# Alternating the high-part and low-part products of the expert weights, k by k, in a streaming-encoder kernel

## The reference, cut to what matters

```python
def peer_ffn(h, w_q, sub_keys, u_tab, v_tab):
    ...
        idx = jnp.take_along_axis(cand_i, best_pos, axis=-1)
        gate = jax.nn.softmax(best_s, axis=-1)
        u = jnp.take(u_tab, idx, axis=0)
        act = jax.nn.gelu(jnp.einsum('td,thkd->thk', hb, u).astype(F32))
        v = jnp.take(v_tab, idx, axis=0)
        return jnp.einsum('thk,thkd->td', (gate * act).astype(hb.dtype), v)
```

## Time and profile before

| | |
|---|---|
| time, median of 3 runs | 1838.51 us (1835.72 to 1839.15) |
| span of the profiled execution | 1830.5 us |
| PE busy | 1796.4 us, 98% of the span |
| DVE busy | 1476.1 us, 81% |
| ACT busy | 1115.6 us, 61% |
| POOL busy | 769.2 us, 42% |
| mean granted TensorE clock | 0.999 of full |
| DMA | 391.70 MB, mean 214 GB/s |

### The profile page before, as it was taken

How to read it: one execution, slowest core, us unless ns; L and a number is a source line. 1 busy time by engine, 2 the same in 40 slices (tenths; PEclk the granted TensorE clock), 3 DMA queues, 4 the chain that set the end, 5 groups by cost and what they waited for, 6 DMA issues and landing times. The chain is left out here.

```text
span 1830.5 us, 38340 instructions
## 1 busy us (share of the span) xinstructions
PE 1796.4 (98%) x11836; PEld 1695.5 (93%) x11836; DVE 1476.1 (81%) x3273; ACT 1115.6 (61%) x2184; POOL 769.2 (42%) x452
## 2 busy tenths in 40 slices
PE   8999999999999999999999999999999999999998
PEld 6889999999999999999978899999999999999998
DVE  4765888988887888888667568889888878888886
ACT  5765566667776555555567555666677765555554
POOL 6545320037766444343064462100476755444430
PEclk9999999999999999999999999999999999999999
DMA  8232266664444899999512323666644448888884
GB/s 319 93 137 94 70 209 206 206 217 154 156 149 152 310 384 387 353 380 365 170 62 93 138 93 108 209 203 206 208 158 149 156 167 336 338 321 321 333 299 148
DMA packets 105485, 391.70 MB, mean 214 GB/s; under 512 B 12288, under 2 KB 16000, under 8 KB 102976
## 3 DMA queue, kind: packets, MB, share of 16 engines
q1 hardware_dynamic: 86336, 322.57, 50.6%
q0 software_dynamic: 19072, 68.23, 9.7%
HBM read 388.86 MB, written 1.05 MB: 213 GB/s over the span
## 5 line engine op out<-in xcount | busy, mean ns | idle before, releaser
L630 PE MATMUL ps<-fhl,wh 128*128 128x448 f32 (+1 forms) x2560 | 542.4, 356 | 4.3 <-DVE ps L1606 4.3
L630 PE MATMUL ps<-ghl,wh 128*128 128x448 f32 x2048 | 462.6, 367 | 1.7 <-DVE wl L1841 0.9
L630 PEld LDWEIGHTS ps<-fhl,wh 128*128 128x128 f32 x2560 | 429.7, 189 | 31.7 <-issue 3.4
L630 PEld LDWEIGHTS ps<-ghl,wh 128*128 128x128 f32 x2048 | 366.3, 189 | 26.3 <-issue 1.3
L1192 ACT ACTIVATE wh<-nat 128x1024 fp32r<-128x1024 f32 x260 | 275.7, 1060 | 177.2 <-PE ps L630 91.6
L1841 DVE TENSOR_TENSOR wl<-nat,wh 128x1024 fp32r<-128x1024 f32 x252 | 307.9, 1222 | 74.2 <-ACT wh L1320 73.7
L611 POOL TENSOR_TENSOR wl<-nat,wh 128x1024 fp32r<-128x1024 f32 x112 | 268.6, 2398 | 115.8 <-ACT wh L1192 115.8
L630 PEld LDWEIGHTS ps<-fhl,wl 128*128 128x128 f32 x2304 | 300.5, 191 | 9.0 <-POOL wl L580 1.0
L630 PE MATMUL ps<-fhl,wl 128*128 128x224 f32 (+1 forms) x2304 | 303.6, 274 | 0.6 <-POOL wl L580 0.6
L1319 ACT ACTIVATE ghl<-grid 128x224 fp32r (+1 forms) x252 | 98.6, 391 | 300.8 <-PE ps L630 287.0
L630 PEld LDWEIGHTS ps<-ghl,wl 128*128 128x128 f32 x2048 | 269.5, 191 | 6.5
(11 more groups left out here) (206 smaller groups left out, 2238.9 us busy)
## 6 DMA issues: line engine op xcount, KB each, us to landing
nat<-in_peer_u SPq DMA_DIRECT2D x256, 512.0 KB
nat<-in_peer_v SPq DMA_DIRECT2D x256, 512.0 KB
grid<-in_peer_wq SPq DMA_DIRECT2D x8, 2048.0 KB, 10.7
grid<-in_w_out SPq DMA_DIRECT2D x2, 4096.0 KB, 12.7
grid<-in_w_in SPq DMA_DIRECT2D x3, 2048.0 KB, 16.0
grid<-in_w_in SPq DMA_DIRECT2D x24, 256.0 KB
grid<-in_bias SPq DMA_DIRECT2D x2, 1664.0 KB, 16.8
grid<-in_w_in SPq DMA_DIRECT2D x2, 1024.0 KB, 23.5
```

Of the source, the lines that this page charges most:

```text
L630: return nc.tensor.matmul(dst, a, b, start=first, stop=last)
```

## The change

In product (U) and block_v (V) one loop over k issues the high product and then the low product of that k. The wait for the rest (rest, or gv_rest) moves from between the two loops to the front of the block. The semaphore high_used of U is still raised by the last high product, which is now the last product but one of the block.

```diff
                         both = ps[:, 4 + b, 0:2 * DT].rearrange("p (a t) -> p a t", a=2)
+                        pe.wait_ge(rest, past[rest] + count * 2 + (2 - 2 * before))
                         for k in range(KD):
                             ins = mm(both, wh[:, b, k * P:(k + 1) * P], fhl[:, :, k, 0:DT], k == 0, False)
-                        ins.then_inc(high_used, 1)
-                        pe.wait_ge(rest, past[rest] + count * 2 + (2 - 2 * before))
-                        for k in range(KD):
+                            if k == KD - 1:
+                                ins.then_inc(high_used, 1)
                             ins = mm(ps[:, 4 + b, 0:DT], wl[:, b, k * P:(k + 1) * P], fh[:, k, 0:DT], False, k == KD - 1)
                         ins.then_inc(prod_done, 1)
...
                         need_high(q, s)
+                        need_rest(q, s)
                         for k in range(KD):
                             high_y(s % 2, k)
-                        need_rest(q, s)
-                        for k in range(KD):
                             ins = rest_y(s % 2, k)
                         ins.then_inc(y_done, 1)
```

## The result

The changed kernel takes 1963.28 us (median of 4 runs, 1961.71 to 1964.08) against 1837.12 us of the kernel before in the same session: a ratio of 1.0694, 95% interval 1.0678 to 1.071, so 126 us slower. The forecast was 1955.5 us in 1925 to 1990. The span of the profiled execution went from 1830.5 to 1961.3 us, at a mean granted clock of 0.999 as before.

A forecast was written before the change was run, and what follows sets the result against it. PE was taken to set the time, busy almost throughout the expert stages. V's 76 and U without gates' 41 made 117 us, added to the 1838.5 us median for 1955.5 us, range 1925 to 1990.

The forecast's parts named there:

- The order costs nothing: U and V: pairs in turn cost 313 ns against 315 grouped, 0 to -8 us at most, taken as 0.
- V, 76 us forecast: V: PE waits for wl at the front, two intervals sum to 5.63 instead of 5.02 us, 0.305 a block.
- T: Moment when a block's last low product starts; in V the next block was to start at T + 0.11 us.
- U without gates, 41 us forecast: U without gates: late high_used delays wh 0.78 us, two intervals sum to 5.61 instead of 5.04, 0.285 a block.
- U with gates, 0 forecast: U with gates: the longer chain stays hidden behind the gates with 0.24 us to spare, 0 us.
- Rival (a): U with gates stalls too, or nat and gathers come late: +14 us each, 1970 to 1984; chance 0.12.
- DMA: Fetches into nat start 0 to 0.8 us later; ACT's waits in V could cost 0 to 14 us, taken as 0.
- (b): V and U: every block pays the whole 0.6 us, 235 us, time 2073; chance 0.04.
- (c): Only one of two stages loses: V alone gives 1914, U without gates alone 1879; chance 0.06.
- (d): V and U: no change, the preparation finishing within T + 2.6 in both stages; chance 0.02.
- (e): Expert blocks: faster, weight loads hide better under products in turn, 37 us less, 1801; chance 0.02.
- (f): Pauses lower the granted clock, 25 us per 10 one-block stretches of V at half clock; chance 0.02.

The follow-up runs named there:

- e3: Kernel before with the waits for the rest at the block's front, products still grouped, high_used raised in mid-block; 1919.87 us, ratio 1.0465.
- e4: Kernel before with products alternating, each low one four k behind its high one, wait for the rest after four high ones; 1850.51 us, ratio 1.009.
- e7: Changed kernel with PE's wait for summed in U put behind those for high_ready and rest; 1952.97 us, ratio 1.0653 to the kernel before.
- e8: Kernel before with the alternating loop and front wait only in the 54 gated blocks of U; 1835.29 us, ratio 0.9999.
- e5: Changed kernel with an unused DVE subtraction between the new wh and wl in V; 1995.68 us, ratio 1.0881 to the kernel before.

## Why the prediction was right, step by step

**The order costs nothing: shown.** In V's block above seven pairs take 783.71 - 781.51 = 2.20 us, 314 ns each, and most blocks of U have 314 too, nearly as read from the last block. The prediction says of that row that every product goes into the bank that the one before has just written. In V only the low ones do, as each k has its own bank; for U, where all 16 share one, it is the changed kernel's trace that shows the price. The runs that separate order and wait agree: V with the wait and without the order (e3) loses all, V with the order and without the early wait (e4) nothing.

**V, 76 us forecast, 80.7 measured.** Chain, mechanism and the half of it a block hold: the constant sum of two intervals in the trace, and the runs with a longer and a shorter chain. The term that was too small is the distance from a block's start to its T, taken as 2.41 from a block that hadn't waited and measured as 2.47 to 2.48; the last block in the earlier trace rows, from which the price of a pair was read, had 2.47. With it the median pair takes 5.68 us and not 5.63. The mean interval of V is 2.861 and 2.849 us in the two layers where 2.815 was forecast, 10 us more in all; but before the change it was 2.528 and 2.536 and not 2.51, 5.5 us more as well, and so the difference was missed by only 4.7 us. The sums of intervals leave at most 0.1 us a pair for DVE's dots and sums.

**U without gates, 41 us forecast, 49.0 and 1.3 measured.** The 49.0 us are the 142 intervals of the table, the 1.3 us the first two of each layer. The steps up to the end of add_halves were read to 0.01 us from a trace that doesn't show them in this order. Two terms were too small: the distance from there to PE, 0.13 taken from a row in which PE had one wait to work off and mostly 0.23 to 0.24 measured with two, and the distance from a block's start to its T, 2.42 taken and 2.48 to 2.50 measured. The median pair takes 5.78 and 5.80 us and not 5.61, half of which on 142 intervals is 13 us; with a few longer ones the stage is 16 us longer than 142 intervals of 2.805 us. That the loss was missed by only 8 us has to do with the other end: before, an interval took 2.575 us in the mean and not the 2.52 read from one block, which leaves 8 us less to lose. Here two errors partly cancelled, and that is luck. e7 checks the first term: the distance falls by 0.19 us and 0.03 come back at the first low product, so half of 0.16 on 142 intervals or 11 us is due; e7 gives back 10.2. The prediction put the two edits in U together. The changed kernel's list of waits tells them apart:

```profile
PE ps L630 <- DVE ps L1605: 21.4, 63, 1.2
...
PE ps L630 <- DVE wl L1600: 2.0, 2, 1.0
```

PE waits for add_halves, for which it waited at the front before as well, and hardly for the rest. The chain that holds it begins at high_used: wh starts at T - 0.44 before, T - 0.10 in e4 and T + 0.34 in the changed kernel, and add_halves ends at T + 2.29, T + 2.62 and T + 3.06, later by the same amounts. The wait at the front alone costs 1.7 us a layer (e3), high_used at half of the way without it 6.6 us (e4). By these rows the wait at the front adds to the late high_used mainly the second wait to work off, an estimated 0.1 us in two intervals; high_used fully late without the front wait wasn't run.

**U with gates, 0 forecast, -1.8 us measured.** Hidden, with POOL's rest ready in time; the small gain is that of the order, 2 ns a pair, as e8 shows. Rival (a) doesn't happen. **DMA**, 0 forecast: ACT's waits for a block of V, 13.9 us in the earlier trace rows, are gone from the changed kernel's list of waits, and the stage sums leave 1.6 us of the span. Rivals (b) to (e) are out with the stage figures and e5, (f) with the granted clock of 1.00 in all three stretches.

**In sum:** 117 forecast, 126 by the runs and 131 by the spans. One execution of the changed kernel has both figures, 1963.07 us and a span of 1961.3, so 1.8 us lie between them; the 8.0 us that the prediction put between span and median were mostly scatter, the profiled execution of before being a quick one. The stages missed the forecast by 12 us, more than the medians show. The Trainium skill's rule on hiding weight loads (TensorE: Matmul & The Clock Gate, "LDWEIGHTS" and Part 2, step 1) would have made a gain plausible; a pair costs 313 to 314 ns in turn and 315 in groups, so no run here shows more of a gain than these 2 ns.

## What to carry to other kernels

When the same two buffers are refilled after use, ask for each operand as late and release it as early as the order of the instructions allows: here two things moved by less than a block's length, in V one wait to the front and in U mainly one release to the end, and turned slack of up to a microsecond into a loss on an engine that had been 98% busy, though its own work cost the same. With two buffers the chain from the end of one block to the start of the next but one sets the sum of two intervals, so a block pays half of what the chain is too long; a row in which an engine already waits that way gives the length of the chain before anything is built, if all terms are taken from that row and the base from the mean of the stage rather than from one block. And of several waits in front of an instruction, put the one that comes last at the end.

## What was not expected of the hardware

PE's start after the semaphore that it waits for last depends on how many waits stand behind that one in its program: after add_halves 0.05 to 0.06 us for none (e7), 0.13 to 0.14 for one (before, e4) and mostly 0.23 to 0.24 for two (changed kernel, e3). They are satisfied before it, and the figures fit their being worked off only then. The number of waits isn't all: after wl in V, with none behind, it is 0.15 us (the earlier trace rows and the changed kernel); why, stays open. And after such a start the first pair of products takes 0.38 us where the later ones take 0.31, both in U and in V: in the changed kernel the second weight load started 0.07 us after the first product (at 784.29) instead of 0.01, as these rows of it show, the first three after a pause and then two within a block:

```profile
784.26 0.19 PEld L630 LDWEIGHTS ps<-ghl,wh 128*128 128x128 f32 x1 [0.56 <-issue]
...
784.36 0.19 PEld L630 LDWEIGHTS ps<-ghl,wl 128*128 128x128 f32 x1
...
784.57 0.27 PE L630 MATMUL ps<-ghl,wl 128*128 128x224 f32 x1
...
784.67 0.37 PE L630 MATMUL ps<-ghl,wh 128*128 128x448 f32 x1
784.68 0.19 PEld L630 LDWEIGHTS ps<-ghl,wl 128*128 128x128 f32 x1
```
